# A transformer block in split fp32r on one core: lambda scalars ahead of the layers, conditioning products spread over four attention stages, their low parts on GpSimd

## The reference

```
lam = exp(sum(lv[0] * lv[1])) - exp(sum(lv[2] * lv[3])) + lam_init
for l in range(2):
    mod   = silu(c)    @ w_ada[l] + b_ada[l]      # 1024 x 6144 weights
    mod_c = silu(c_ctx) @ w_ada[l] + b_ada[l]
    sh1, sc1, gt1, sh2, sc2, gt2 = split(mod, 6)
    a_x = rms_norm(h, g_mix[l]) * (1 + sc1) + sh1
    y   = mixer(a_x, ...)          # Fourier mix, differential attention
                                   # (weights softmax - lam * softmax),
                                   # neighbourhood attention, gated sum, w_out
    h   = h + gt1 * y
    f_x = rms_norm(h, g_ffn[l]) * (1 + sc2) + sh2
    h   = h + gt2 * conv_ffn(f_x)
```

## Time and profile before

| | us |
|---|---|
| median of 3 runs | 3031.41 |
| lowest and highest | 3023.72, 3038.21 |
| the profiled execution | 3040.34 |
| its span, first to last instruction | 3038.5 |
| PE busy | 2787.8 (92%) |
| DVE busy | 1754.9 (58%) |
| ACT busy | 1406.3 (46%) |
| POOL busy | 57.2 (2%) |

### The profile page before, as it was taken

How to read it: one execution, slowest core, us unless ns; L and a number is a source line. 1 busy time by engine, 2 the same in 40 slices (tenths; PEclk the granted TensorE clock), 3 DMA queues, 4 the chain that set the end, 5 groups by cost and what they waited for, 6 DMA issues and landing times.

```text
span 3038.5 us, 42732 instructions
## 1 busy us (share of the span) xinstructions
PE 2787.8 (92%) x17980; PEld 2422.3 (80%) x17980; DVE 1754.9 (58%) x2928; ACT 1406.3 (46%) x2258; POOL 57.2 (2%) x75
## 2 busy tenths in 40 slices
PE   4997899998999997989989979989998999789999
PEld 2875576676777775877789979987998999667999
DVE  5255634345666665454568756656566657565565
ACT  5245635433444444464655544445444545433443
POOL 1000000000000000000000000000000000000000
PEclk7998999999999998999999989999999999776999
DMA  6223422121444432223345545542455555200454
GB/s 224 66 90 111 145 76 67 53 95 64 153 139 136 142 132 97 91 98 104 112 141 192 167 144 183 175 130 83 154 183 164 169 194 167 86 28 1 153 181 139
DMA packets 337391, 382.16 MB, mean 126 GB/s; under 512 B 7408, under 2 KB 301296, under 8 KB 337200
## 3 DMA queue, kind: packets, MB, share of 16 engines
q1 hardware_dynamic: 334656, 370.37, 37.0%
q0 software_dynamic: 2544, 9.06, 0.9%
HBM read 378.36 MB, written 1.05 MB: 125 GB/s over the span
## 4 chain that ended last, share of the span: by engine, by line
PE 80%; DVE 10%; ACT 7%; issue 2%; DMA 1%; POOL 0%; DVEq 0%; ACTq 0%; POOLq 0%
PE PS L1026 21%; PE PS L1028 20%; PE PS L1027 20%; PE PS L1142 2%; ACT WH L1304 2%; DVE WL L1585 2%; DVE TMP L1621 2%; PE PS L1043 1%; PE PS L1044 1%; PE PS L1045 1%; PE PS L1075 1%; PE PS L1157 1%; PE PS L1282 1%; PE PS L1125 1%; DVE RS L1613 1%
## 5 line engine op out<-in xcount | busy, mean ns | idle before, releaser
L1585 DVE TENSOR_TENSOR WL<-RAWB,WH 128x1024 fp32r<-128x1024 f32 (+1 forms) x709 | 845.9, 1203 | 659.2 <-ACT WH L1304 658.1
L1026 PE MATMUL PS<-AH,WH 128*128 128x256 f32 (+1 forms) x3072 | 980.7, 319 | 55.3 <-DVE AL L1626 44.0
L1027 PE MATMUL PS<-AL,WH 128*128 128x256 f32 (+1 forms) x3072 | 963.7, 314 | 0.0
L1028 PE MATMUL PS<-AH,WL 128*128 128x256 f32 (+1 forms) x3072 | 963.1, 314 | 0.0
L1304 ACT ACTIVATE WH<-RAWB 128x1024 fp32r<-128x1024 f32 (+1 forms) x709 | 725.0, 1036 | 349.3 <-PE PS L1028 308.5
L1026 PEld LDWEIGHTS PS<-AH,WH 128*128 128x128 f32 x3072 | 589.6, 192 | 126.8 <-DVE AL L1626 45.5
L1028 PEld LDWEIGHTS PS<-AH,WL 128*128 128x128 f32 x3072 | 589.8, 192 | 34.8
L1027 PEld LDWEIGHTS PS<-AL,WH 128*128 128x128 f32 x3072 | 590.6, 192 | 32.2 <-issue 0.2
L1026 PE MATMUL PS<-BH,WH 128*128 128x256 f32 (+1 forms) x1504 | 480.7, 320 | 7.0 <-DVE BL L1722 3.0
L1027 PE MATMUL PS<-BL,WH 128*128 128x256 f32 (+1 forms) x1504 | 463.1, 308 | 0.0
L1028 PE MATMUL PS<-BH,WL 128*128 128x256 f32 (+1 forms) x1504 | 462.8, 308 | 0.0
(11 more groups left out here) (259 smaller groups left out, 2824.7 us busy)
## 6 DMA issues: line engine op xcount, KB each, us to landing
RAWB<-in_f_in SPq DMA_DIRECT2D x88, 1024.0 KB, 5.0
RAWB<-in_w_in SPq DMA_DIRECT2D x52, 1024.0 KB, 4.9
RAWB<-in_w_ada SPq DMA_DIRECT2D x48, 1024.0 KB, 5.2
RAWB<-in_w_up SPq DMA_DIRECT2D x44, 1024.0 KB, 5.2
RAWB<-in_f_out SPq DMA_DIRECT2D x40, 1024.0 KB, 4.9
RAWB<-in_w_down SPq DMA_DIRECT2D x20, 1024.0 KB, 5.0
RAWB<-in_sb_qkv SPq DMA_DIRECT2D x12, 1024.0 KB, 4.9
RAWB<-in_w_out SPq DMA_DIRECT2D x8, 1024.0 KB, 5.1
```

The lines of the kernel that those rows point to most:

```text
L1026: pe.matmul(out, h, xh[:, 0:T], start=k == 0, stop=False)
L1027: pe.matmul(out, h, xl[:, 0:T], start=False, stop=False)
L1028: i = pe.matmul(out, l, xh[:, 0:T], start=False, stop=k == g.kt - 1)
L1585: dve.tensor_tensor(c.part("WL", p), c.raw(p.slab)[:, k0:k1, c0:c1], c.part("WH", p).bitcast(F32), ALU.subtract).then_inc(up("lo", ("lo", ...
```

## The change

Three things. The `lam` steps of both layers now stand ahead of the first conditioning products, each with scratch columns and a result column of its own. The slabs of `w_ada` carry a mark `by`: those ahead of everything keep DVE for the low part, all others have it made by POOL (`by="pool"`), which signals on a semaphore of its own. And `ada` is called elsewhere: layer 0's chunks 16 to 47 stay in its da; layer 1's chunks 0 to 15 go into the na of layer 0, 16 to 31 into the da of layer 1, 32 to 47 into the na of layer 1; none is left in the FFN.

```diff
-    def slab(self, w, k0, kt, c0, cols, cuts=()):
+    def slab(self, w, k0, kt, c0, cols, cuts=(), by="dve"):
...
-    def ada(self, l, n0, n1):
+    def ada(self, l, n0, n1, by="pool"):
...
-        lb = self.banks.take()
-        self.add("lam", (l,), b=lb)
-        self.banks.give(lb, ("lam_exp", l))
...
-        ada = self.ada(0, 16, 48) if l == 0 else iter(())
+        ada = self.ada(l, 16, 48 if l == 0 else 32)
         filler = itertools.chain(da_qk(1), self.mixed(merge(0, "w_a", 0, lambda k: ("fa", l, k)), ada))
         self.weave(self.run_units([(h, qt) for h in range(4) for qt in range(nq)], da1), filler, 4 * nq,
-                   4 + 16 + (16 if l == 0 else 0))
+                   4 + 16 + (16 if l == 0 else 8))
...
-        filler = itertools.chain(na_qk(1), merge(1, "w_b", 4, lambda k: ("db", l, k)))
-        self.weave(self.run_units([(h, qt) for h in range(8) for qt in range(nq)], na1), filler, 8 * nq, 4 + 16)
+        ada = self.ada(1, 0, 16) if l == 0 else self.ada(1, 32, 48)
+        filler = itertools.chain(na_qk(1), self.mixed(merge(1, "w_b", 4, lambda k: ("db", l, k)), ada))
+        self.weave(self.run_units([(h, qt) for h in range(8) for qt in range(nq)], na1), filler, 8 * nq, 4 + 16 + 8)
...
-        self.weave(self.ffn(f"c{l}", ("w_up", l), ("w_down", l), T, lambda k: ("xlo", b, k), "up_conv", "res", (l, 5), nrm),
-                   self.ada(1, 0, 48) if l == 0 else iter(()), 32, 24)
+        self.finish(self.ffn(f"c{l}", ("w_up", l), ("w_down", l), T, lambda k: ("xlo", b, k), "up_conv", "res", (l, 5), nrm))
...
         self.add("start")
-        self.finish(self.ada(0, 0, 16))
+        for l in range(2):
+            lb = self.banks.take()
+            self.add("lam", (l,), b=lb)
+            self.banks.give(lb, ("lam_exp", l))
+        self.finish(self.ada(0, 0, 16, "dve"))
...
+        elif s.kind == "split" and s.p.slab.by == "pool":
+            p = s.p
+            k0, k1, c0, c1 = p.cut
+            on.wait_ge(*at("hi", p.p))
+            pool.tensor_tensor(c.part("WL", p), c.raw(p.slab)[:, k0:k1, c0:c1], c.part("WH", p).bitcast(F32),
+                               ALU.subtract).then_inc(up("lo_pool", ("lo", p.p)), 1)
...
+            at_ = 20 + 4 * id[0]
+            on.wait_ge(*at("side", "consts"))
             on.wait_ge(*at("lam_pp", *id))
-            pe.matmul(c.bank(s.b)[:, 0:2], ones[0:64, :], c.m["ST"][0:64, 20:22], start=True, stop=True).then_inc(
+            pe.matmul(c.bank(s.b)[:, 0:2], ones[0:64, :], c.m["ST"][0:64, at_:at_ + 2], start=True, stop=True).then_inc(
```

More of the change, by code:

```diff
@@ L135, with __init__ @@
 class Slab:
-    def __init__(self, j, w, k0, kt, c0, cols, cuts):
+    def __init__(self, j, w, k0, kt, c0, cols, cuts, by):
         self.j, self.w, self.k0, self.kt, self.c0, self.cols, self.cuts = j, w, k0, kt, c0, cols, cuts
-        self.first = None
+        self.first, self.by = None, by
 class Piece:
@@ L211, in run_units @@
             yield
[L215 removed]
+    def slab(self, w, k0, kt, c0, cols, cuts=(), by="dve"):
         j = len(self.slabs)
[L217 removed]
+        s = self.known[j] if self.known else Slab(j, w, k0, kt, c0, cols, list(cuts), by)
         self.slabs.append(s)
@@ L316, in ada @@
             for half in range(2):
-                s = self.slab(("w_ada", l), 0, 8, (c + 2 * half) * 128, 256, [(0, 4, 0, 256), (4, 8, 0, 256)])
+                s = self.slab(("w_ada", l), 0, 8, (c + 2 * half) * 128, 256, [(0, 4, 0, 256), (4, 8, 0, 256)], by)
                 for i in range(2):
@@ L1348, in scalar_program @@
             on.wait_ge(*at("lam_sum", *id))
-            act.activation(ST[:, 22:24], c.bank(s.b)[:, 0:2], ACT.Exp).then_inc(up("acted", ("lam_exp",) + id), 1)
+            act.activation(ST[:, 22 + 4 * id[0]:24 + 4 * id[0]], c.bank(s.b)[:, 0:2], ACT.Exp).then_inc(up("acted", ("lam_exp",) + id), 1)
         elif kind == "ev":
@@ L1580, in vector_program @@
             c.ev.when[("mark", "dve", id)] = (m["sem"]["vec"], c.ev.count.get("vec", 0))
-        elif kind == "split":
+        elif kind == "split" and s.p.slab.by == "dve":
             p = s.p
@@ L1630, in vector_program @@
             lv = c.sm(f"lam{l}")[0:64, :].rearrange("p (a b) -> p a b", b=2)
-            dve.tensor_tensor(ST[0:64, 20:22], lv[:, :, 0], lv[:, :, 1], ALU.mult).then_inc(up("vec", ("lam_pp", l)), 1)
+            a = 20 + 4 * l
+            on.wait_ge(*at("side", "small"))
+            dve.tensor_tensor(ST[0:64, a:a + 2], lv[:, :, 0], lv[:, :, 1], ALU.mult).then_inc(up("vec", ("lam_pp", l)), 1)
             on.wait_ge(*at("lam_exp", l))
-            dve.tensor_scalar(LM[:, 0:1], ST[:, 23:24], ST[:, 22:23], -(0.8 - 0.6 * math.exp(-0.3 * l)), ALU.subtract,
+            dve.tensor_scalar(LM[:, 4 + l:5 + l], ST[:, a + 3:a + 4], ST[:, a + 2:a + 3], -(0.8 - 0.6 * math.exp(-0.3 * l)), ALU.subtract,
                               ALU.add).then_inc(up("vec", ("lam", l)), 1)
@@ L1673, in vector_program @@
             on.wait_ge(*at("da_rec", *id))
-            dve.tensor_tensor(ST[:, 8 + col:9 + col], ST[:, 11 + col:12 + col], LM[:, 0:1], ALU.mult).then_inc(
+            dve.tensor_tensor(ST[:, 8 + col:9 + col], ST[:, 11 + col:12 + col], LM[:, 4 + id[0]:5 + id[0]], ALU.mult).then_inc(
                 up("vec", ("da_lam",) + id), 1)
@@ L1943, in build @@
                    G1=sb("G1", [128, 2, 8, 2]), G2=sb("G2", [128, 2, 8, 2]), ST=sb("ST", [128, 32]),
-                   LM=sb("LM", [128, 4]), SC=sb("SC", [128, 32], F32R), EPS=sb("EPS", [128, 4]), RAWB=sb("RAWB", [128, NR, SLAB]),
+                   LM=sb("LM", [128, 8]), SC=sb("SC", [128, 32], F32R), EPS=sb("EPS", [128, 4]), RAWB=sb("RAWB", [128, NR, SLAB]),
                    WH=sb("WH", [128, NW, PIECE], F32R), WL=sb("WL", [128, NW, PIECE], F32R))
         mem["banks"] = [ctx.enter_context(nc.psum_tensor(f"PS{i}", [128, 512], F32)) for i in range(8)]
-        mem["sem"] = {n: sem(n) for n in ("acc", "hi", "acted", "lo", "vec", "xlo_pool")}
+        mem["sem"] = {n: sem(n) for n in ("acc", "hi", "acted", "lo", "lo_pool", "vec", "xlo_pool")}
         mem["rawsem"] = [sem(f"raw{i}") for i in range(NR)]
```

## The result

The changed kernel took **3131.1 us** (median of 4 runs, 3126.9 to 3140.7) against 3030.8 for the kernel before in the same comparison: ratio **1.0335** (95% interval 1.0301 to 1.0370). The forecast was 3032, with a range up to 3072: it missed by 99 us, on the slow side. The profiled execution took 3130.0 us, span 3128.2, which is 89.7 above the span before.

What follows compares the result with a forecast made beforehand. PE, busy 92% of the span, was taken as the bound; -57.6 (FFN), -5.3 (lambda), +50.0 (moved products) and +3 +3 +4 +3 (waits) summed to 0, so 3032 us was forecast, range 2998 to 3072.

Steps and rivals of the forecast that it cites:

- point 5: Both layers' da and na: waits around conditioning pieces on four slots, +3, +3, +4 and +3 us.
- The walk: One merge round without attention: at 512 columns waits add 3.3 us with DVE, 6.6 with POOL.
- Rival B: Shared port and slot ring become the bound: +94 us uncovered, +47 half covered over 80 pieces; 3066 us, chance 0.27.
- Point 1: FFN of layer 0: conditioning products leave, -50.0 us of work and -7.6 idle, -57.6 in all.
- Point 2: Lambda moved out of the layers: norms 4.7 and 2.6 us shorter, small charges at the head, -5.3 together.
- Point 3: na of layer 0, da and na of layer 1: 16 more chunks each on PE, +50.0 us.
- Point 4: A 1024-column low part takes POOL 2.35 us against DVE's 1.22, and locks DVE's operations with two SBUF inputs meanwhile.
- The signs that were named: Included PE's waits for POOL's `WL` in layer 1's da and na, 10 to 25 us; layer 0's FFN about 360.

Runs made afterwards that it cites:

- experiment 2: The changed kernel with all low parts made by DVE instead of POOL; 3089.7 us, ratio 1.0184 to the kernel before.
- experiment 6: The changed kernel with low parts on DVE, merge and conditioning products taking turns two units at a time (pairs); 3042.2 us, ratio 1.0044.
- experiment 7: The changed kernel, low parts kept on POOL, merge and conditioning products taking turns two units at a time (pairs); 3074.6 us, ratio 1.0137.
- experiment 11: The changed kernel with low parts on DVE, turns of two units, and the hook `self.tick()` removed from `ada`; 3030.7 us, ratio 0.9984.
- experiment 9: The kernel before with conditioning products listed two units at a time (pairs); 3019.0 us, ratio 0.9939.
- experiment 1: The kernel before with the lambda steps ahead of the layers and nothing else; 3030.2 us, ratio 0.9994.
- experiment 15: The kernel before with conditioning weights' low parts on GpSimd and an unused tile ahead of `WH` and `WL`; 3016.3 us, ratio 0.9949.
- experiment 13: The kernel before with one unused tile of 240 columns ahead of `WH` and `WL`, nothing else; 3002.1 us, ratio 0.9886.
- experiment 12: The kernel before with three dummy GpSimd subtractions beside each of 80 pieces, their scratch tile ahead of `WH` and `WL`; 3006.0 us, ratio 0.9895.
- experiment 14: The kernel before with lambda ahead of the layers, conditioning products two units at a time, unused tile ahead of `WH` and `WL`; 2974.8 us, ratio 0.9815.
- experiment 17: The changed kernel with the unused tile ahead of `WH` and `WL`; 3101.4 us, ratio 1.0239.

## Why the prediction was wrong, point by point

**The failed step is point 5, the waits around the conditioning pieces**, and in it the sentences that attention's matmuls "fill part of the waits" and "half stays". It gave +10 for the three stages that got 16 chunks each and +3 for da of layer 0. Measured are +102 beyond the moved work, and +13 (8 in the first line, which has lambda's gain of 4.7 in it).

The mechanism itself was in point 5: a gate product frees the slot of a conditioning piece, and behind it come ACT's high part and POOL's low part. The walk gave 6.6 us a round at 512 columns and 10.3 at 256 (26.5 less 16.2), with nothing covered: 26.4, 13.2, 20.6 and 20.6 us in the four stages, 81 in all. PE's waits for POOL's low parts are 29.1, 19.1, 18.9 and 17.9, 85 in all. So attention covered none of it to speak of. That the two sums agree so well is in part luck: for DVE the same walk gives 35 us, and experiment 2 has 61.

**The clock was left out of the sum.** 40 of the 102 us are PE's own instructions made longer, at .86 to .92 granted clock where they ran at .96 to 1.00. Each term of point 5 counted the wait alone.

By experiments, in ratios of 1% = 30 us, of the change's 3.35%, taken away one after the other:
- 1.5% (46 us): low parts on GpSimd (experiment 2); 0.9% if it goes after the next (experiments 6 and 7). Rival B priced this at +94 uncovered and +47 half covered, and the number is near. But B put it in place of all waits, and its 3066 is 65 us short as well.
- 1.4% (42 us): turns that hold a slot over two conditioning pieces (experiment 6). Point 5 had this wait for the gate's slot, but took it as given by the four slots. No rival said that the order of the turns makes it, or that it can be mended. The four low parts that DVE made in a row, after a wait, fit it: slots coming free together.
- 0.6% (18 us): the hook (experiment 11). In point 5 it stood nowhere.
- Taken together these leave the spread at 0.9984, 5 us under the kernel before, near to the forecast of no change. That is in part luck: 18 us of it are what pairs give the kernel before too, in da of layer 0 (experiment 9). Beside a kernel with lambda and pairs the spread still costs 17 us (experiment 11).

**Point 1** (FFN of layer 0, -57.6): right. It is -60.0 between the same two results; busy time fell by 50.5 (50.0 said) and idle time by 9.5 (7.6 said), the bound that was named for all idle time gone (59.9).

**Point 2** (lambda): right in the norms, in mechanism and in size; that the -5.3 arrive in the total isn't shown (experiment 1). The changed kernel, DVE's reciprocal of the first norm, ACT's first `u` result, and both again in layer 1:

```profile
55.67 3.35 DVE L1624 RECIPROCAL RS<-RS 128x512 f32<-128x512 f32 x1 [10.45 <-ACT RS L1344]
...
75.45 0.60 ACT L1376 ACTIVATE F<-PS 128x512 f32<-128x512 f32 x1 [2.39 <-PE PS L1037]
...
1180.51 3.35 DVE L1624 RECIPROCAL RS<-RS 128x512 f32<-128x512 f32 x1 [2.60 <-ACT RS L1344]
...
1200.32 0.38 ACT L1376 ACTIVATE F<-PS 128x256 f32<-128x256 f32 x1 [2.44 <-PE PS L1037]
```

19.8 us in both layers, against 24.5 and 22.1: -4.7 and -2.3, as said (-4.7 and -2.6). At the head ACT's first split starts at 10.52, slab 1's at 16.93 (17.22 before), and the norm starts 1 us later:

```profile
10.46 0.17 ACT L1360 ACTIVATE ST<-PS 128x2 f32<-128x2 f32 x1 [0.98 <-PE PS L1092]
10.52 1.99 ACT L1315 ACTIVATE WH<-RAWB 128x1024 fp32r<-128x1024 f32 x2
16.93 2.00 ACT L1315 ACTIVATE WH<-RAWB 128x1024 fp32r<-128x1024 f32 x2 [4.41 <-DMA RAWB<-in_w_ada]
```

**Point 3** (+50.0): the same matmuls; at full clock it stands (50.5 left the FFN).

**Point 4** (2.35 us for a low part on POOL, and the lock): right. The changed kernel's sources, ns min/median/max:

```profile
L999 POOL TENSOR_TENSOR WL<-RAWB,WH x80: 2338/2382/3353, 184.1 to 1556.0; 128x1024 fp32r<-128x1024 f32 x80
```

```profile
L1596 DVE TENSOR_TENSOR WL<-RAWB,WH x629: 558/1225/3392, 11.6 to 3117.5; 128x1024 fp32r<-128x1024 f32 x152, 128x512 fp32r<-128x512 f32 x6
```

DVE's longest low part is 3.39 us (near 3.5 said) where it was 1.23. The Trainium skill's "Perfetto Trace Analysis" ("Optimizing Scalar/DVE Operations") warned that work moved between DVE and GpSimd might not help, and here it didn't: 46 us. But its reason, the port, had 3 to 5 of about 20 us where a GpSimd that only holds DVE was run by itself (experiment 15). The rest is left to the low part's own time on the way from a weight's high part to its product, 2.38 us and not 1.22. How the 46 us of the spread placement divide is open.

**The signs that were named**: PE's waits for POOL's low parts in da and na of layer 1 came to 36.8 us (10 to 25 said). That was the one sign off, and the one that mattered. The FFN's held: 357.0 us from 805.1 on, the place of the earlier trace rows's 738, with 0.4 us of idle time.

## What to carry to other kernels

Before counting idle time, or other work in the stage, as cover, write down for each new piece which slot it needs, who holds that slot, and what is queued ahead of its split. If slots are given by number, use pieces in the order of their numbers. And where PE's clock falls behind waits, price a wait at more than its length: here 61.6 us of new idle time came with 40 us of slower matmuls.

## What the runs showed of the hardware that was not expected

**The place of the weight tiles changes the matmuls' pace.** One steady stretch of the last feed-forward stage (three rounds, the same work), in the kernel before and in that with the unused tile (experiment 13):

```profile
2882.21:2984.74 102.53, 102.53 (x866) 102.53 (x865) 62.57 (x84) 45.14 (x61) 0.00 (x0) 1.00 0.56 185
```

```profile
2852.91:2950.83 97.92, 97.92 (x867) 97.92 (x866) 62.56 (x84) 45.16 (x61) 0.00 (x0) 1.00 0.58 194
```

PE is busy throughout, the granted clock is 1.00 in both, and a matmul takes 118.4 or 112.9 ns. But the place alone doesn't fix the pace. The kernels of experiments 12, 14, 15 and 17 share one layout (with the 8 columns of `LM`). The feed-forward stage near the middle takes 206.4, 205.8, 205.7 and 213.0 us in them, 212.8 in experiment 13 and 214.2 in the kernel before; the last one takes 219.5, 224.5, 217.6 and 219.4, against 217.5 and 226.2. These are single profiled executions, and the six runs of experiment 13 reach from 2976.0 to 3004.1 us. Which tile, bank or reader lies behind it wasn't found.

**A stage that nothing touched varies by 15 us.** The compressed-attention stage near the end took 194.9 us at clock .68 in the kernel before and 179.7 at .76 in the changed one; the kernel before with the tile behind `WL` had 179.8 at .76 as well, and experiment 2 had 185.7 at .72. Each is a single profiled execution; how often each length occurs wasn't counted. This, and that the kernel before was profiled in an execution 9 us above its median, must be kept in mind where the profiles' difference of 89.7 stands beside the medians' 100.

**An operation with one tile as input was held too.** L1725 multiplies softmax weights in place by a column (its longest 2.40 us, its median 0.49; longest 0.49 in the kernel before); the prediction had counted such scaling among those that POOL's work holds, and the rows agree.
